# Three retention heads' states computed late instead of two, the first expert pair's gather and state products in another order, and the ninth weight chunk loaded in four parts

## What is computed

```
proj = xn @ w_in                     # q, k, v, g, gates and conv inputs, 1024 x 11264
r, S = retention(q, k, v)            # per head: out = (q k' * decay) v ;  S_final = (k * k_decay)' v
merged = sig(ga)*o_a + sig(gb)*o_b   # o_a: gated short convolution, o_b: normed, gated retention
h = x + merged @ w_o
logits = rmsnorm(h) @ w_router ;  4 of 32 experts per token
h = h + sum over chosen experts of gate * ffn_e(h)     # w_e1 1024 x 2048, w_e2 1024 x 1024
y = rmsnorm(h)
outputs: y, last conv rows, S_final of the prompt (4 heads of 256 x 512), updated decode states
```

## Time and profile before

| | us |
|---|---|
| median of 3 runs | 1426.85 |
| the profiled execution | 1426.69 |
| its span | 1425.1 |
| PE busy, share of the span | 1353.2, 95% |
| DVE, ACT, POOL busy | 387.4, 252.3, 94.2 |
| mean rate of all transfers | 365 GB/s |

### The profile page before, as it was taken

The page is one execution under the profiler, slowest core; times in us unless marked ns, Lnnn a source line. Parts: engine busy times, 40 slices in busy tenths (PEclk is TensorE's granted clock), DMA queues, the critical chain, the costliest instruction groups (busy, mean ns, idle before and its releaser), DMA issues.

```text
span 1425.1 us, 17289 instructions
## 1 busy us (share of the span) xinstructions
PE 1353.2 (95%) x7193; PEld 704.2 (49%) x7193; DVE 387.4 (27%) x711; ACT 252.3 (18%) x375; POOL 94.2 (7%) x163
## 2 busy tenths in 40 slices
PE   8999999999999999999989989889899898998997
PEld 6667668788887543443333334333333333332342
DVE  4235443642501331221221212212121122111223
ACT  1233343321000431111111101111011111101112
POOL 1122212210000210000000000000000000000000
PEclk9999999999999999999999999999999999999999
DMA  9987879874433589999999999999999999999997
GB/s 349 373 317 276 306 250 344 284 269 156 154 127 155 222 376 428 434 429 430 433 431 432 431 431 432 431 431 433 430 431 433 431 430 434 430 430 435 423 428 293
DMA packets 43298, 519.94 MB, mean 365 GB/s; under 512 B 5194, under 2 KB 5754, under 8 KB 21460
## 3 DMA queue, kind: packets, MB, share of 16 engines
q1 hardware_dynamic: 29136, 471.67, 79.1%
q0 software_dynamic: 12576, 44.62, 9.1%
q10 hardware_dynamic: 1540, 2.99, 0.5%
HBM read 497.63 MB, written 21.67 MB: 364 GB/s over the span
## 4 chain that ended last, share of the span: by engine, by line
PE 71%; DMA 26%; DVE 1%; SPq 1%; issue 0%; ACT 0%; DVEq 0%; ACTq 0%
PE bank L1846 24%; PE bank L1533 23%; DMA arena<-in_w_pairs 15%; DMA ring<-in_w_pairs 12%; PE bank L1811 4%; PE bank L1581 4%; PE bank L1797 3%; PE bank L1898 2%; PE bank L1676 2%; PE bank L1550 1%; SPq L632 1%; PE bank L1642 1%; PE bank L1844 1%; PE bank L1807 1%; PE bank L1875 1%; PE bank L1863 1%
## 5 line engine op out<-in xcount | busy, mean ns | idle before, releaser
L1846 PE MATMUL bank<-ring,arena 128*64 128x512 f32 x1536 | 348.4, 606 | 34.7 <-DMA ring<-in_w_pairs 34.7
L1533 PE MATMUL bank<-arena,ring 128*128 128x264 f32 x1472 | 335.7, 388 | 0.0
L1533 PEld LDWEIGHTS bank<-arena,ring 128*128 128x128 f32 x1472 | 277.5, 190 | 52.0 <-issue 6.0
L1846 PEld LDWEIGHTS bank<-ring,arena 128*64 128x64 f32 x1536 | 112.5, 139 | 247.7 <-issue 229.2
L1898 PE MATMUL bank<-ring,arena 128*64 128x512 f32 x768 | 172.6, 595 | 3.1 <-DMA ring<-in_w_pairs 3.0
L1846 PE MATMUL bank<-arena 128*64 128x512 f32 x512 | 118.4, 610 | 13.2 <-DMA arena<-in_w_pairs 13.2
L1898 PEld LDWEIGHTS bank<-ring,arena 128*64 128x64 f32 x768 | 55.1, 137 | 101.4 <-issue 99.6
L1463 DVE TENSOR_SCALAR arena<-bank 128x512 f32<-128x512 f32 x32 | 22.1, 691 | 272.5 <-PE bank L1846 272.5
L1846 PEld LDWEIGHTS bank<-arena 128*64 128x64 f32 x512 | 37.0, 140 | 87.8 <-issue 87.8
L1482 DVE COPY arena<-bank 64x512 f32<-64x512 f32 x32 | 21.9, 683 | 181.4 <-PE bank L1898 181.4
L1453 DVE TENSOR_TENSOR hs<-hs,bank 128x256 f32<-128x256 f32 x16 | 6.7, 421 | 225.3 <-PE bank L1807 225.3
(11 more groups left out here) (241 smaller groups left out, 995.5 us busy)
## 6 DMA issues: line engine op xcount, KB each, us to landing
ring<-in_w_pairs SPq DMA_DIRECT2D x59, 4096.0 KB, 28.9
arena<-in_w_pairs SPq DMA_DIRECT2D x19, 4096.0 KB, 27.1
ring<-in_w_mixer SPq DMA_DIRECT2D x58, 1024.0 KB, 8.6
ring<-in_w_pairs SPq DMA_DIRECT2D x26, 2048.0 KB, 12.7
arena<-in_state_ret POOLq DMA_DIRECT2D x32, 512.0 KB, 7.4
out_ret_sample<-arena POOLq DMA_DIRECT2D x32, 512.0 KB, 6.2
arena<-in_w_pairs SPq DMA_DIRECT2D x8, 2048.0 KB, 16.2
arena<-v_decode POOLq DMA_DIRECT2D x32, 256.0 KB, 6.9
```

The costliest lines, as they stand in the source:

```text
L1533: ins = pe.matmul(bank[:, 0:T], weight(n + k // 4, k % 4)[:, 128 * j:128 * (j + 1)], rhs[:, k, :], start=k == 0, stop=k == KD * groups - 1)
L1846: ins = pe.matmul(out, xgT[:, k, 64 * e:64 * (e + 1)], held(n, 2 * D * (k % W1_KS) + c), start=False, stop=k == KD - 1)
```

## The change

- `DEFERRED` becomes (0, 1, 2). Heads 0, 1 and 2 are saved; head 3, the last, makes its state in the mixer. Its `kt`, `out` and `st` now come right after its values and ahead of its `g` projections.
- Only head 0's k is turned and scaled in the mixer. Heads 1 and 2 save k unturned, and PE turns it later (`turn_kept`), with ACT scaling it in `ktok_half`.
- Head 0's four products take the place between mixer and experts; ACT issues its output of 0.5 MB there. Head 1's k is turned in the first pair after four k-steps of expert 0, and its products stand between the halves of expert 1's first layer, where the gather was; the gather comes after the second half. Head 2's k is turned and multiplied in the second pair, between the parts of expert 1's work.
- POOL reads head 2's v back into a part of `hx` and half its k into `router`, after their last use.
- The ninth chunk of the first pair goes as four 0.5 MB transfers. Each is released by two of the eight products (128x512, two column halves) that read the first chunk.
- `qv` has three places instead of two, and the mixer's list is written anew from these rules, so the decode steps stand elsewhere in it.

```diff
-DEFERRED = (2, 3)
+DEFERRED = (0, 1, 2)
...
-        main.extend([(("v", h, 2), 2.2), (("vs", h), 0.0), (("v", h, 0), 7.0), (("qs", h), 0.0), (("kt", h), 0.5),
-                     (("sc", h), 1.4), (("v", h, 1), 7.0)])
-        proj(("g", h))
-        main.append((("out", h), 2.7))
-        main.append((("save", h), 0.0) if h in DEFERRED else (("st", h), 3.6))
+        main.extend([(("v", h, 2), 2.2), (("vs", h), 0.0), (("v", h, 0), 7.0), (("qs", h), 0.0)])
+        if h == 0:
+            main.append((("kt", h), 1.0))
+        main.extend([(("sc", h), 1.4), (("v", h, 1), 7.0)])
+        if h in DEFERRED:
+            proj(("g", h))
+            main.extend([(("out", h), 2.7), (("save", h), 0.0)])
+        else:
+            main.extend([(("kt", h), 1.0), (("out", h), 2.7), (("st", h), 3.6)])
+            proj(("g", h))
...
+                    elif (first or alone and half == 0) and n == WIDE_SLOTS:
+                        if not first:
+                            is_free(n)
+                        for f in range(W2_FS):
+                            if first and f < W2_FS - 1:
+                                sp.wait_ge(part_used, f + 1)
+                            elif first:
+                                is_free(n)
+                            sp.dma_start(dst[:, D * f:D * (f + 1)], mine[:, D * f:D * (f + 1)])\
+                                .then_inc(early_in if f < W2_FS - 1 else slot_in[at], 16)
...
             ac.activation(route[:, 3:6, :], route[:, 3:6, :], ACT.Exp).then_inc(gate_exp, 1)
+            ac.wait_ge(kept_read, 2)
+            ac.dma_start(o["ret_prompt"][0, 0, 0].rearrange("(k p) v -> p k v", p=128), st_kept[0]).then_inc(st_out, 16)
             split(1, 1, 0, D // 2)
             split(1, 1, D // 2, D)
+            bank = read(ac, ("kt", 1))
+            for t in range(2):
+                ins = ktok_half(1, t, bank)
+            empties(ins, ("kt", 1))
             ac.wait_ge(rest_ready, len(SPLITS))
             state_half(1, 0)
             state_half(1, 1)
...
+                            if first and e == 0 and 0 < 2 * k + q < 2 * W1_KS:
+                                ins.then_inc(part_used, 1)
...
                 if first:
-                    first_layer(0, range(-1, KD))
+                    first_layer(0, range(-1, 4))
+                    pe.wait_ge(kept_in[1], 48)
                     pe.wait_ge(added, ADDS * it + ADDS)
-                    final_states(4, 8)
+                    fills(turn_kept(1, fill(pe, ("kt", 1))), ("kt", 1))
+                    first_layer(0, range(4, KD))
...
-                if first:
-                    pe.wait_ge(kept_read, 2 * len(DEFERRED))
-                    pe.wait_ge(rest_ready, len(SPLITS))
...
+                if first:
+                    was_read(pe, ("kt", 1))
                 first_layer(1, range(-1, 4))
-                gather(g + 1)
+                if first:
+                    final_states(1, 0, 4)
+                else:
+                    gather(g + 1)
                 pe.wait_ge(pgT_ready, it + 1)
                 turn_acts(0)
+                if alone:
+                    pe.wait_ge(kept_in[2], 48)
+                    turn_kept(2, psum[LATE_BANKS[1]]).then_inc(kT_turned, 1)
                 first_layer(1, range(4, KD))
+                if first:
+                    pe.wait_ge(kept_read, 4)
+                    pe.wait_ge(rest_ready, len(SPLITS))
+                    gather(g + 1)
+                if alone:
+                    pe.wait_ge(late_ktok, 2 * r + 2)
+                    for g in range(2):
+                        for t in range(2):
+                            ins = pe.matmul(psum[LATE_BANKS[g]][:, :], k_kept[2][:, t, 128 * g:128 * (g + 1)],
+                                            v_kept[2][:, t, :], start=t == 0, stop=t == 1)
+                        ins.then_inc(late_state, 1)
```

More of the change, by code:

```diff
@@ L251, in mixer_order @@
             continue
-        if ends:
+        if ends and not (ends[0][0] == "ss" and event[0] == "proj" and event[1][0] in ("q", "k") and event[2] == 2):
             order.append(ends.pop(0))
@@ L321, in bank_plan @@
     use("count", 1)
-    for i, h in enumerate(DEFERRED):
-        use(("st", h, 0), (0, 3)[i])
-        use(("st", h, 1), (4, 2)[i])
+    use(("st", 0, 0), 0)
+    use(("st", 0, 1), 4)
+    use(("kt", 1), 3)
+    use(("st", 1, 0), 6)
+    use(("st", 1, 1), 7)
     return plan, count
@@ L378, in build @@
         v_sb = view(11872, 2, DV)
[L379 removed]
+        values = [v_sb, view(14000, 2, DV), v_sb, view(14000, 2, DV)]
         vs_sb = view(12896, 128)
@@ L487, in build @@
         rT_ready, ctok_out, merged_ready = sem("rT_ready"), sem("ctok_out"), sem("merged_ready")
-        saved, kept_in, kept_read = sem("saved"), sem("kept_in"), sem("kept_read")
+        saved, kept_read = sem("saved"), sem("kept_read")
+        kept_in = [sem(f"kept_in{h}") for h in DEFERRED]
+        kT_turned, late_ktok, late_state, late_read = sem("kT_turned"), sem("late_ktok"), sem("late_state"), sem("late_read")
         kept_out = sem("kept_out")
@@ L832, in _ @@
                     if t < 2:
-                        if t == 0 and h >= 1:
-                            if h == H - 1:
-                                ac.wait_ge(st_out, 16 * (H - len(DEFERRED)))
-                            else:
-                                was_filled(ac, ("st", h - 1, 1))
+                        if t == 0 and h >= 2:
+                            was_filled(ac, ("out", h - 2, 1))
+                            ac.wait_ge(saved, 32 * (h - 1))
                         empties(ac.activation(values[h][:, t, :], bank[:, :], ACT.Copy), event)
@@ L877, in _ @@
                         bank = read(ac, use)
-                        if g == 0 and h >= 1:
-                            ac.wait_ge(st_out, 16 * h)
+                        if g == 0:
+                            was_filled(ac, ("out", H - 2, 1))
+                            ac.wait_ge(saved, 32 * len(DEFERRED))
                         empties(ac.activation(st[:, g, :], bank[:, :], ACT.Copy), use)
@@ L988, in state_half, with ktok_half @@
                 ac.activation(st_kept[i][:, g, :], read(ac, ("st", DEFERRED[i], g))[:, :], ACT.Copy).then_inc(kept_read, 1)
+            def ktok_half(i, t, bank):
+                return ac.activation(k_kept[i][:, t, :], bank[:, DK * t:DK * (t + 1)], ACT.Copy,
+                                     scale=cst[:, C_KDEC + 2 * i + t:C_KDEC + 2 * i + t + 1])
             ac.wait_ge(xn2_ready, 4)
@@ L1023, in _ @@
+            with ac.Fori(0, rounds) as r:
+                expert_pair(r, 0, first=True)
+                expert_pair(r, 1, late=True)
+                with ac.Fori(2, PAIRS) as pair:
+                    expert_pair(r, pair)
             ac.activation(stat[:, 13:14], stat[:, 12:13], ACT.Sqrt)
@@ L1211, in _ @@
                     g = which[0]
-                    v.wait_ge(saved, 32 * len(DEFERRED))
+                    was_filled(v, ("st", H - 1, 1))
+                    v.wait_ge(st_out, 16)
                     def tap(j, i):
@@ L1258, in _ @@
                             was_filled(v, ("out", H - 1, 1))
+                            v.wait_ge(saved, 32 * len(DEFERRED))
                             own(v.memset(U[:, :, 0:2], 0.0))
@@ L1706, in route_logits, with final_states @@
                 return ins
-            def final_states(first, last):
-                pe.wait_ge(kept_in, 32 * len(DEFERRED))
+            def final_states(i, first, last):
+                pe.wait_ge(kept_in[i], 16 * (2, 3)[i])
                 for step in range(first, last):
-                    i, g, t = step // 4, step // 2 % 2, step % 2
+                    g, t = divmod(step, 2)
                     use = ("st", DEFERRED[i], g)
@@ L1718, in final_states, with turn_kept @@
                         fills(ins, use)
+            def turn_kept(i, bank):
+                for t in range(2):
+                    for half in range(2):
+                        ins = pe.transpose(bank[:, DK * t + 128 * half:DK * t + 128 * (half + 1)],
+                                           kT_kept[i][half][:, 128 * t:128 * (t + 1)], ident)
+                return ins
             bank = fill(pe, ("wo", 2, 0))
@@ L1821, in slot_ready @@
                     at = slot_of(half, n)
+                    if first and n == WIDE_SLOTS:
+                        pe.wait_ge(early_in, 16 * (W2_FS - 1) * (r + 1) + 16 * early_base)
                     if n % 2 == 0:
```

124 lines of the change are left out of this document (77 added, 47 removed).

## The result

| | before | after |
|---|---|---|
| median | 1428.42 us (5 runs) | 1436.11 us (5 runs, 1432.44 to 1437.59) |
| the profiled execution | 1426.69 | 1437.59 |
| its span | 1425.1 | 1435.8 |

The ratio is 1.0051, with a 95% interval of 1.0041 to 1.0062: slower by 0.5%. In a second set it was 1.0051 again (1.0038 to 1.0065). I had forecast 1427.2, in a range that ended at 1430.8. A ratio here is estimated from the runs of its set and is not the quotient of the two medians. One of the six runs of whole9_again, 1456.73 us at a granted clock of 0.939, was in a slower state that this program can fall into, and it is left out of every median and ratio.

The account below looks back on a forecast made before the run. Until about 510 us PE bounds the kernel, then one gapless transfer stream. Stream +4.3 and mixer -3.9 gave +0.4 on 1426.69, 1427.1; with the median 0.16 above, the forecast was 1427.2 us, range 1422.8 to 1430.8.

Parts of the forecast that it names:

- PE's lateness at T: Second pair: PE 10.0 us late releasing the two chunks for T, the 4 MB transfer issued at 602.46 before.
- Two regimes, the end set by the stream: Whole kernel: until about 510 us the end moves with PE, then with one gapless transfer stream to 1410 us.
- The mixer, -3.9: Mixer: 4.5 us of PE work goes, a 1.1 us wait comes, a 0.5 us wait goes; sum -3.9.
- The standstill, 5.7 us: First pair, behind head 1's products: PE stands still 5.7 us until ACT's chain gives expert 0's turned activations.
- Its rival, that ACT would be done under PE's work: First pair: no standstill, PE only 0.2 us late there and 4.3 in the second pair; 1422.7 us, chance 0.14.
- the rival on ACT's chain: First pair: each of two table loads keeps ACT 1.4 us longer, PE stands 8.5 us; 1430.0 us, chance 0.02.
- The rest of the first pair is the same work: First pair behind the standstill: work unchanged at the clock of before, so PE is 5.9 us late at its end.
- The gaps: Stream: gaps of 2.2 us at the 539.01 transfer, 2.6 at 594.98, 4.3 at 602.46; only the largest counts.
- The slack of 5.7 at T: Second pair, transfer of 602.46: 5.7 us of lateness is free, so 10.0 moves the stream by 4.3.
- The quarters and the traffic, swallowed: Ninth chunk's quarters gain at most 1.4 us, added traffic costs at most 2.7; later gaps swallow both.
- The signs: Expected: 5 to 6 us PE idle, share dips near 536 to 538 and 600; wrong if last quarter issued by 508 or later.

Follow-up runs that it names:

- whole9_again: The changed kernel with the ninth chunk in one transfer as before, run beside the changed kernel again: 1434.38 us, ratio 1.0040 to the kernel before.
- states_behind: The changed kernel with ACT's two copies of head 1's state moved behind the first pair's sigmoid: 1425.26 us, ratio 0.9981 to the kernel before.
- reorder_only: The kernel before with only the first pair's order changed (head 3's four products between expert 1's halves, gather behind): 1433.92 us, ratio 1.0043.
- behind_whole9: states_behind with the ninth chunk again in one transfer: 1425.57 us, ratio 0.9984 to the kernel before.
- delay_7: The kernel before with eight unused products added in the second pair behind expert 1's first layer: 1430.98 us, ratio 1.0012.
- delay_11: The kernel before with twelve unused products added in the second pair: 1434.47 us, ratio 1.0040.
- quarters_only: The kernel before with only the ninth chunk split into four transfers released by quarters: 1430.15 us, ratio 1.0015.

## Why the prediction was wrong

The mechanism was forecast and came; three terms of the sum had the wrong size. PE's lateness at T was put at 10.0 and was 12.3, mostly because the prediction kept the full clock behind the standstill. The mixer's gain was put at 3.9 and was 2.6, and the slack at T at 5.7 and was 4.9. Step by step, in the order of the prediction:

1. **Two regimes, the end set by the stream.** Right. The stream as a whole moved, and nothing behind it: from the end of the last weight transfer to the end of the span it is 14.9 us before and 15.3 after. The two spans differ by 10.7 us: S is 0.4 later (1.35 from ahead of the change, less 0.94 of the mixer), the stream behind it 10.0, the end 0.4; the excess of 0.1 is rounding.
2. **The mixer, -3.9.** Right in sign, short in size. From the row at 37.57 to S it is 457.8 us before; in states_behind, at full clock too, it is 493.06 - 37.91 = 455.15, so -2.6. In the shown execution after it is only -0.94, since the clock fell at 490 us (last section). The new waits at head 3 came as forecast (0.34 and 0.54 against 1.1), and the 0.5 of the earlier trace rows went. The other 1.3 of the forecast's 3.9 lies in small pieces of the new list that I have not traced to rows; PE at head 3:

```profile
196.28 0.67 PE L1685 MATMUL bank<-arena 128*128 128x256 f32 x2 [0.34 <-ACT arena L869]
...
198.36 0.70 PE L1685 MATMUL bank<-arena 128*128 128x256 f32 x2 [0.54 <-ACT arena L885]
```

3. **The standstill, 5.7 us.** Right: 5.5, at its place, by its chain. Its rival, that ACT would be done under PE's work, was wrong for the changed kernel, and states_behind is that rival built: I had given it 1422.7, it took 1425.26. For the rival on ACT's chain, the trace has both table loads at 1.28 and no drain behind them. The 8.5 us that I had estimated from the Trainium skill's figure ("ScalarE: Activation LUTs", section "What ACT_TABLE_LOAD costs") did not come.
4. **"The rest of the first pair is the same work", 5.9 late at its end.** Here the working failed first. "I keep the clock of before" was wrong, and so, for this kernel, was the remark that the clock plays no part: the clock falls with the standstill, and the turning and 32 products behind it cost 0.5 + 1.3 = 1.8 us more than in states_behind. With a rest of 0.6 that I have not traced PE was 8.1 us late where the transfer of 546.10 is released, and 12.3 at T instead of 10.0.
5. **The gaps.** I priced the transfers of 539.01, 594.98 (its issue is at 594.64) and 602.46 and passed over the one of 546.10, with 3.3 us of slack. By the forecast's own 5.9 it would have given 2.6 and changed nothing. Measured, the transfer of 539.01 is issued 4.7 late instead of 2.8 and lands 3.5 late where I had 2.2, and that of 546.10 lands 5.5 late. So most of the gap is open before T (reorder_only, which has only this part: 6.2 of the 7.4).
6. **The slack of 5.7 at T.** Nearly right: 4.9. The 6.7 by the Trainium skill's 2.0 us ("DMA: Bandwidth & Descriptors", section "Anatomy of one DMA") is further off; that section's figure is a fit for transfers that GpSimd issues, and these are SyncE's, which left 2.4 to 2.5 us beside the bytes (last section).
7. **The quarters and the traffic, swallowed.** In the changed kernel the ninth chunk lands 1.2 us earlier after S, near the 1.4, and the gaps swallow it, as forecast. That the quarters could cost time was no term of the sum. The traffic shows at the transfer behind S, which lands 1.1 us later after S in the changed kernel and 2.1 in states_behind; U in states_behind is not late, so it costs nothing there.
8. **The signs.** The standstill, a gap in the stream and the fall of the times to landing came. The second dip of the transfers' share, expected about 600 us, did not show: it is 0.99 or more from 600 to 620. But the last quarter was issued at 510.06, past the 508 that I had set as a sign of being wrong. Counted from S the first quarter came 2.6 us earlier, as forecast; what was missing is the mixer's gain and the 1.35 us ahead of the change.

In sum: 10.0 - 5.7 - 3.9 = +0.4 was forecast, and 12.3 - 4.9 - 2.6 = +4.8 is what the same sum gives with the measured terms. The lateness has 2.3 of the difference, the mixer 1.3, the slack 0.8. The medians show 6.4 to 7.7. Of the rest up to 2.6 are the slow single transfers above; what remains I put down to the scatter of executions, which no run here takes apart.

That scatter also bent the base. Part of it is likely the fall of the clock at 490 us that some executions have and others not: behind_whole9 has six runs from 1424.54 to 1425.57 and five from 1427.09 to 1427.28, some 2 us apart, where that fall costs 1.7. That is argued from the size, since a kernel has one traced execution here, or two. The profiled execution of before, 1426.69, is at the low end: in the later sets the kernel before has medians from 1428.40 to 1429.31. I had taken the shown three runs' word for it, which put the forecast some 2 us too low by itself.

## What to carry over

Where work is moved on one engine, follow the program of the engine that answers it: ACT's two copies stood in program order ahead of the sigmoid, and moving them behind it turned a loss of 0.5% into a gain of 0.2%. A transfer stream has a slack at every release; at T, where it was measured, lateness was free up to that slack and paid in full above it. So list every release behind the place of the change, not only the ones that look tight. And price a standstill of PE above its length, for the lower clock that follows it.

## What the runs showed of the hardware

- A standstill of 5.5 us, with full clock ahead of it, came with a granted clock of 0.50 (1.2 GHz) in the 5 us window in which it ended and 0.82 in the next, and cost 1.8 us on top.
- The granted clock also falls without any idle time of PE. In 490 to 495 us it was 0.66 in the changed kernel, where the row of PE (eight products, start and us) is

```profile
490.32 5.38 PE L1741 MATMUL bank<-ring,arena 128*128 128x512 f32 x8
```

and in the kernel before, in the shown execution, with a clock of 1.00:

```profile
491.60 3.68 PE L1676 MATMUL bank<-ring,arena 128*128 128x512 f32 x8
```

It is no part of the change: variants of both kernels show it in some profiled executions (delay_7 and delay_11, whose edit lies in the second pair, and reorder_only, of those built on before) and not in others (quarters_only, states_behind). It costs 1.7 us each time: 456.85 instead of 455.15 us from the row of the first products to S in the kernels built on the changed one, and 459.5 instead of 457.8 in those built on before. What brings it on is open.
- In an idle queue 2 MB landed after 7.3 us (after, 544.15) and 4 MB after 12.2 (T in delay_11). Beside the bytes at 431 GB/s that leaves 2.4 to 2.5 us, not the 3.0 that I had used. By it the slack at T would be 18.5 - 12.2 = 6.3, and T itself lands just that much less late than it is issued. But the transfer behind T then takes 11.1 us from landing to landing in delay_11, where 9.7 are usual: the 1.4 us between 6.3 and 4.9 are lost in the transfer behind the gap.
